# Attention probabilities: turned by a product with a diagonal of reciprocal sums instead of being scaled in memory and transposed

## The reference, cut to what matters

```
s = einsum('bhqd,bhkd->bhqk', qi, k) * scale            # then the causal mask
p = softmax(s, axis=-1)
o = einsum('bhqk,bhkd->bhqd', p, v)
...
o = g[..., 0:1] * o_cmp + g[..., 1:2] * o_slc + g[..., 2:3] * o_win     # g = sigmoid(gate_logits), per query and head
...
o = o1.astype(f32) - lam * o2.astype(f32)               # differential heads
```

## Time and profile before

| | us |
|---|---|
| median of 3 timed runs | 3105.85 (3104.79 to 3110.17) |
| the profiled execution's own time | 3100.32 |
| its span | 3098.6 |
| attention of layer 0, first scores to the last ones' masks | about 523 to 668 |
| attention of layer 1 | about 1610 to 1742 |
| dilated attention | about 2350 to 2421 |

### The profile page before, as it was taken

The page is one execution under the profiler, slowest core; times in us unless marked ns, Lnnn a source line. Parts: engine busy times, 40 slices in busy tenths (PEclk is TensorE's granted clock), DMA queues, the critical chain, the costliest instruction groups (busy, mean ns, idle before and its releaser), DMA issues.

```text
span 3098.6 us, 42427 instructions
## 1 busy us (share of the span) xinstructions
PE 2925.9 (94%) x16328; PEld 2228.0 (72%) x16328; DVE 1791.9 (58%) x2566; ACT 920.8 (30%) x1679; POOL 1124.4 (36%) x661
## 2 busy tenths in 40 slices
PE   7999999999999999999999999999998677999888
PEld 6888867677888878887676778887797676555444
DVE  7766685757656676667757665666555765112111
ACT  3222232543222232223225432223335751111111
POOL 3443354454434434433544543443443550000000
PEclk9999999999999999999999999999999888999999
DMA  5222222013222222221210132222230005999997
GB/s 205 88 95 102 82 82 82 1 38 114 94 102 100 83 102 84 99 102 61 93 72 2 43 121 102 102 83 97 82 123 21 21 4 216 404 423 423 423 424 316
DMA packets 45077, 411.47 MB, mean 133 GB/s; under 512 B 4992, under 2 KB 5248, under 8 KB 12032
## 3 DMA queue, kind: packets, MB, share of 16 engines
q1 hardware_dynamic: 44784, 408.03, 33.9%
q0 software_dynamic: 144, 1.38, 0.1%
HBM read 407.29 MB, written 2.10 MB: 132 GB/s over the span
## 4 chain that ended last, share of the span: by engine, by line
PE 79%; DVE 9%; DMA 5%; issue 4%; ACT 3%; POOL 1%; SPq 0%; DVEq 0%; ACTq 0%; POOLq 0%
PE banks L1642 10%; PE banks L1641 10%; PE banks L1640 9%; PE banks L1918 6%; PE banks L1605 5%; PE banks L1474 5%; PE banks L1651 5%; PE banks L1652 5%; PE banks L1653 5%; DMA experts<-moe_w 4%; PE banks L1553 3%; PE banks L1929 3%; PE banks L1689 2%; PE banks L1717 2%; PE banks L1702 2%
## 5 line engine op out<-in xcount | busy, mean ns | idle before, releaser
L809 POOL TENSOR_TENSOR ffn_parts<-ring,ffn_parts 128x2048 fp32r<-128x2048 f32 x87 | 403.0, 4633 | 732.4 <-ACT ffn_parts L917 732.4
L2230 DVE SCALAR_TENSOR_TENSOR x<-banks,x 128x512 f32<-128x512 f32 x704 | 473.0, 690 | 301.0 <-PE banks L1653 300.1
L1642 PE MATMUL banks<-x_parts_high,ffn_parts 128*128 128x512 f32 x672 | 263.8, 393 | 0.0
L1641 PE MATMUL banks<-x_parts_high,ffn_parts 128*128 128x512 f32 x672 | 262.8, 391 | 0.0
L1640 PE MATMUL banks<-h_lo,ffn_parts 128*128 128x512 f32 x672 | 262.2, 390 | 0.0
L1640 PE MATMUL banks<-x_parts_low,ffn_parts 128*128 128x512 f32 x672 | 261.8, 390 | 0.0
L1642 PE MATMUL banks<-h_hi,ffn_parts 128*128 128x512 f32 x672 | 261.4, 389 | 0.0
L1641 PE MATMUL banks<-h_hi,ffn_parts 128*128 128x512 f32 x672 | 261.4, 389 | 0.0
L917 ACT ACTIVATE ffn_parts<-ring 128x2048 fp32r<-128x2048 f32 x88 | 168.6, 1915 | 289.3 <-PE banks L1642 287.8
L814 POOL TENSOR_TENSOR ffn_parts<-ring,ffn_parts 128x1024 fp32r<-128x1024 f32 x88 | 212.8, 2418 | 104.8 <-ACT ffn_parts L923 104.6
L1918 PE MATMUL banks<-experts,mix 128*64 128x256 f32 x1520 | 191.6, 393 | 16.1 <-DMA experts<-moe_w 16.1
(11 more groups left out here) (395 smaller groups left out, 6699.5 us busy)
## 6 DMA issues: line engine op xcount, KB each, us to landing
ring<-ffn_w SPq DMA_DIRECT2D x87, 1536.0 KB, 6.5
experts<-moe_w SPq DMA_DIRECT2D x47, 2048.0 KB, 18.7
experts<-moe_w SPq DMA_DIRECT2D x48, 1024.0 KB, 18.1
ring<-mix_w SPq DMA_DIRECT2D x24, 1536.0 KB, 6.4
ring<-second_w SPq DMA_DIRECT2D x16, 1536.0 KB, 6.5
expert_table<-moe_w SPq DMA_DIRECT2D x16, 1024.0 KB, 14.9
expert_h<-moe_w SPq DMA_DIRECT2D x16, 1024.0 KB, 20.1
expert_table<-moe_w SPq DMA_DIRECT2D x16, 512.0 KB, 11.6
```

The costliest lines, as they stand in the source:

```text
L809: pool.tensor_tensor(s[:, 1], w, s[:, 0].bitcast(F32), ALU.subtract).then_inc(up_split, 1)
L1641: mm(bank[n % 2 + 2 * a], w[:, 0, a, k], hi[:, k], start=False, stop=False)
L1642: last = mm(bank[n % 2 + 2 * a], w[:, 1, a, k], hi[:, k], start=False, stop=k == KC - 1)
L2230: V.scalar_tensor_tensor(x[:, q], bank[4 + q % 4], scale, x[:, q], ALU.mult, ALU.add).then_inc(down_used, c.one(down_used))
```

## The change

The probabilities are no longer scaled in place. POOL builds, for each step and head, a 128x128 matrix `inverse` with the query's factor (reciprocal of the sum, times gate) on the diagonal: the identity matrix multiplied by one number per partition. `turn` multiplies the unscaled probabilities, again as the weights, with this matrix as the moving operand, by an ordinary f32 product in place of the transpose instruction. The result is the transposed and scaled block. `inverse` has room for two steps, so POOL also waits until the turn of step a-2 is done (pT_ready) before it writes that of step a.

```diff
+    inverse = sb("inverse", 4 * P).rearrange("p (b e n) -> p b e n", b=2, e=2)
...
         def attention(pairs, lows=()):
+            turns = c.at.get(pT_ready.name, 0)
             for a in range(NT * len(pairs)):
                 if lows and a in LOWS_AT:
                     out_low(lows[LOWS_AT.index(a)])
                 u, i = pairs[a // NT], row_of(pairs, a)
                 pool.wait_ge(den_ready, c.next(den_ready))
+                pool.wait_ge(pT_ready, max(turns + 2 * (a - 1), 0))
                 for e in range(2):
-                    v = PROBS[:, a % 4, e, 0:u["tiles"][e][i]["n"]]
                     by = 2 * (a % 4) + e
-                    pool.tensor_scalar(v, v, RDEN[:, by:by + 1], u["gate"][e][i] if u["gate"][e] else 1.0, ALU.mult, ALU.mult).then_inc(scaled_ready, 1)
+                    pool.tensor_scalar(inverse[:, a % 2, e], ident, RDEN[:, by:by + 1], u["gate"][e][i] if u["gate"][e] else 1.0,
+                                       ALU.mult, ALU.mult).then_inc(scaled_ready, 1)
+            c.skip(pT_ready, 2 * NT * len(pairs))
...
                     for j in range(t["blocks"]):
-                        last = nc.tensor.transpose(bank[2 + e][0:t["rows"], P * j:P * j + P],
-                                                   PROBS[:, a % 4, e, P * j:P * j + t["rows"]], ident)
+                        last = mm(bank[2 + e][0:t["rows"], P * j:P * j + P], PROBS[:, a % 4, e, P * j:P * j + t["rows"]],
+                                  inverse[:, a % 2, e], start=True, stop=True)
                     last.then_inc(pT_ready, 1)
```

## The result

| | before | changed |
|---|---|---|
| median, us | 3105.32 (3104.17 to 3110.17, 4 runs) | 3158.08 (3151.94 to 3162.03, 4 runs) |
| profiled execution, span | 3098.6 | 3160.3 |

The ratio is 1.017 with a 95% interval of 1.0154 to 1.0187: slower by 53 us, where 3160 was forecast. The profiled execution of the changed kernel took 3162.03 us, the longest of its four, and that of before was short for its kernel, so their 61.7 us of difference are some 9 more than that of the medians.

The account below looks back on a forecast made before the run. The prediction took PE to bound the kernel, 93 to 94% busy in the layers' attentions. 60.8 - 12 + 13.7 - 8 = 54.5 us on the median of 3105.85 gave 3160 us, range 3130 to 3186.

Parts of the forecast that it names:

- PE's part: At the turn, 696 transposes become two-record products, each 0.107 us more: 60.8 us in layers, 13.7 in dilated attention, 74.5 total.
- What is hidden: PE's waits at turn and scores absorb part of the longer turns: 12 us in the layers, 8 in the dilated attention.
- the lower bound: Least cost: all 48.1 us of PEld-row waits in the attentions absorbed, leaving 26.4 us.
- Stages: The three attention stretches grow by some 24, 24 and 6 us (layer 0, layer 1, dilated), nothing elsewhere.
- POOL and the added wait: POOL's changed work and its wait for the turn two steps before, counted as 0 since nobody waits for POOL.
- Full price: Rival at the attentions: nothing is absorbed, +74 to +88 us, 3180 to 3194; chance 0.12.
- Deep absorption: Rival: scores, maximum and exponential loop holds the attentions, turn time is filler; +26 to +40 us, 3132 to 3146; chance 0.10.
- Not slower: Rival at the turn: a product costs one record like a transpose; 3106 or 1 to 5 us less; chance 0.04.
- The factor of four: Rival at the turn: a product costs four transposes, 0.467 us; +216 us, 3322 us; chance 0.03.

Follow-up runs that it names:

- e1: Kernel before with only the turn made a product, by the identity matrix, POOL scaling in memory as before: 3158.7 us against 3103.26, ratio 1.0174.
- e6: Kernel before with each transpose issued twice into the same place, no product: 3152.48 us against 3104.06, ratio 1.0153.
- e3: Kernel before with the change in the attentions of the first block (the two layers) alone: 3148.35 us against 3103.26, ratio 1.0145.
- e4: Kernel before with the change in the dilated attention alone: 3109.01 us, ratio 1.0016.
- e2: Changed kernel with the transpose by the identity matrix put back, POOL still building the matrices: 3102.1 us against 3103.26 before, ratio 0.9996.
- e7: Changed kernel with room for three steps of matrices in place of two: 3154.52 us against 3104.06 before, ratio 1.0161.
- e8: Kernel before with POOL's scaling in memory cut to one column per head: 3102.94 us against 3104.06, ratio 0.9995.
- e5: Changed kernel with the turn's two operands in the rounded type fp32r: 3190.84 us against 3104.06 before, ratio 1.0269.
- e9: e5 with a moving operand of 256 columns for the first three blocks of each head: 3106.99 us against 3103.52 before, ratio 1.001.
- e10: e5 with each rounded product issued twice into the same place: 3229.18 us against 3103.52 before, ratio 1.0409.

## Why the prediction was right

**PE's part.** The two records for each product came as said. The growth for each block was a little short. The term took 0.117 us for a transpose and 0.224 for a product, a growth of 0.107. Measured over a turn of four blocks it is 0.97 / 8 = 0.121. The reason is the start of a turn. Read record by record, the turn of eight transposes at 2381.34 has its second record 0.164 us behind the first and all others 0.109 apart, also from one head to the other. The average of 0.117 had this longer first distance in it. The product rows that I compared it with stand in the middle of a series and have none. But the product's turn has one too, and a longer one: 0.213 at 2421.85, then 0.112. The 0.049 between them is about what the load grew by (192 ns in place of 140), the cost at the head of a group that the prediction saw and counted at nothing. It is paid, though once a turn and not once a head. With all sizes of turns, the turns at full clock grew by 0.25, 0.49, 0.71 and 0.96 us for one to four blocks. With 50, 26, 26 and 42 such turns (the compressed steps are among the 50) the term should have been 84 us, not 74.5.

**What is hidden.** 20 us were taken. PE's row lost 19.5 us of turn waits, 11.4 of them in the layers and 8.1 in the dilated attention, near the 12 and 8 of the prediction, and 21.6 us of all its idle time. The balance of the medians, 84 less 53, asks for some 30. The likely reason is that PE's own row hides part of a wait under the drain of the matmul before. The PEld rows agree: their waits at the turn and at the scores fell by 7.0 + 7.3 + 10.2 + 2.9 + 2.5 = 29.9 us. That these are the very 30 is not shown, since other idle time on the PEld row changed as well. I had used these rows only for the lower bound. The two errors, 10 us each, have opposite signs; the 3160 is partly luck, the mechanism is not (e1, e6).

**Stages.** 24, 24 and 6 us were forecast; the profiled pair shows 26, 26 and 5, and e3 and e4 measured 45 for the two layers and 6.

**POOL and the added wait.** Counted at nothing; e2 (-1 us), e7 and e8 (-1 us) bear it out. POOL did begin to wait for PE, for 128 us, as an engine with slack may.

**The rivals.** Full price (3180 to 3194): excluded by the time, and by the waits that shrank. Deep absorption (up to 3146): excluded for the changed kernel; with 36% of the added work hidden more was absorbed than I said, but not that much. Not slower: excluded by the record count. The factor of four: measured is 1.99 / 1.02 = 1.95 for a whole turn of f32 operands at full clock. The Trainium skill ("TensorE: Matmul & The Clock Gate", Terms) gives four; no run here shows it.

## What to carry to other kernels

To turn a block by an ordinary f32 product cost nearly twice the TensorE time of the transpose instruction here (1.99 against 1.02 us for eight blocks). Folding a scaling into it can pay only if the engine that did the scaling is waited for, and a run with that scaling cut to one column (e8) tells this before anything is rebuilt. Price a series of instructions from the start of one group to the start of the next engine step, since the longer first distance is then in both sides. After a change to what TensorE executes, read the granted clock before the busy share.

## What the runs showed of the hardware

The granted clock can stay at half for long while TensorE is busy 10.00 of 10 us (e5), and at full clock the records of the versions that lose it look like those of the others. On the turn's line, at full clock, the median record of a transpose lasts 273 ns, of an f32 product 275, of a rounded product of 128 columns 276 (e5) and of one mostly of 256 columns 281 (e9); inside a turn they start 0.109, 0.112, 0.112 and 0.118 us apart. Whole turns agree: six of the rounded ones take 0.80 us to the next group, six transposes 0.81. With the first two and the last the attentions of the layers run at 2.4 GHz, but for dips of 3 to 10 us; with 128 rounded columns they stand at 1.2 GHz for up to 109 us on end (e5) and 102 (e10), and adding useless columns gives 84 us back (e9). What about the wider product keeps the clock isn't shown: its columns, its slightly longer turn and the repeated operand were changed together, and a wide operand of real data was not tried. Nor is it shown why e10's clock returns in the middle of the attention.

In e5 the fall begins at the head of the attention, where PE stands 1.60 us for the first exponentials. This alone doesn't decide it. The kernel before stands there as long and keeps 1.00 in layer 0. In the changed kernel's layer 0 the clock falls too, and comes back at once; the columns are those of the stretches above (clock third from the end):

```profile
527.00:531.00 4.00, 2.83 (x13) 2.30 (x13) 1.49 (x4) 2.44 (x9) 0.79 (x3) 0.70 0.00 0
531.00:533.00 2.00, 2.00 (x15) 2.00 (x14) 0.59 (x2) 1.51 (x8) 0.64 (x2) 0.74 0.00 0
533.00:543.00 10.00, 9.32 (x95) 7.35 (x93) 5.39 (x10) 2.67 (x11) 2.87 (x8) 1.00 0.01 2
```

Transposes among products run at full clock here. The attentions of the layers in the kernel before, with 568 transposes, stand at 1.00, and e6 with twice as many has 1.00 around its turn of 16 at 644.70. The Trainium skill ("TensorE: Matmul & The Clock Gate", Part 4) says that the full clock doesn't engage for transpose mode; for transposes between products this case disagrees, and of transposes alone no run here shows anything.
